# One 512-column product in place of two of 256 in the interior groups of a two-block kernel

## Chip, cores and metric

One core of a Trainium2 chip runs the whole program. The metric is device time in microseconds for one execution; less is better.

## The reference

Two transformer blocks over the same 256 tokens of 1024 features, batch 1, in fp32. The first: RMS norm, one wide input projection, gated linear attention with four heads in chunks of 64, dilated window attention with three groups of four heads, sigmoid gates and an output product, an MLP with squared ReLU (1024 to 4096 to 1024), a gated per-layer embedding, a norm. The second has two layers: SwiGLU with 2816 inner features, a convolution module (width 31) in layer 0 or multi-head latent attention in layer 1, a second SwiGLU, and a final norm. What matters here is its dense part, products of activations (256 tokens) with weights that are read once:

```
h @ w_in[i]
jnp.square(jax.nn.relu(h2 @ w_mlp1[i])) @ w_mlp2[i]
(jax.nn.silu(h @ w1) * (h @ w3)) @ w2         # four times
```

## The kernel before

**Products in three terms.** TensorE works on operands of type fp32r. To keep fp32's accuracy each operand is held as two: a rounded high part and the rest. Weights stand in `wsplit[:, slot, kk, h, :]`, activations in `xa[:, k, h, :]` or `parts[:, c, h, :]`, where h is 0 for high and 1 for rest, and the two halves lie next to each other. A product is high x high + high x rest + rest x high, three matmuls of 256 columns that add into the same place in PSUM (L535). In layout "F" the weights are stationary and the 256 tokens move; in layout "T" (the v projections) the activations are stationary and 256 weight columns move.

**Phases, groups, blocks.** The dense part is a list of phases (`add(...)`, class `Phase`). A phase's output is cut into groups of 256 output columns; a group sums over K in blocks of up to four k of 128 rows. K8 is two blocks of 4, K22 eight blocks of 3 or 2, K32 eight blocks of 4. For each k of a block and each c, one of two column blocks of 128, PE issues the three matmuls (`product_group`), after waiting for the block's weights (`lo_done`); the last of a block counts `used`. Group number G, counted through all phases, writes PSUM `ps[:, G % 2, c, 0:256]`, one bank for each c, and before it PE waits until group G - 2 has been taken (`val_done`). Groups with their kind of evacuation: gla_q and gla_k 2 each, gla_v 4, nine att phases 2 each ("keep", and "keep_tok" for v), mlp1 16 ("relu2"), mlp2 4 ("resid", K32), four up phases ffn1_up0, ffn2_up0, ffn1_up1, ffn2_up1 22 each ("swiglu"), four down phases 4 each ("resid", K22), and hr, gates, y_gla, y_att, w_out, w_pg, w_pp, pw1, pw2, mla_a, mla_kr, the uq and ukv phases, w_o and ha.

**The weights' way.** SP loads a block of up to 512 KB into one of 8 slots (L481) once the block 8 before it is used. ACT rounds it to the high part (L843, `round_block`), 5 blocks ahead of the group it belongs to; DVE subtracts to get the rest (L1057, `rest_block`), 4 blocks ahead. Both do this in the order written out in their loops: for each block of a group `ahead`, then the evacuation of that group.

**Evacuation.** DVE waits for `used` of the group's last block and reads the sum from PSUM: "keep" scales it by `rstd` (L1113), "keep_tok" by a column (L1125); a swiglu pair takes the even group as `t1 = sum * rstd` (L1138), ACT makes the silu (L901), and the odd group is multiplied with it (L1162) and split into high and rest in `parts` (L1085, L1086); "relu2" takes the maximum with 0 into `val` (L1168), squares it (L1170) and splits; "resid" of mlp2 and the down phases scales into `val` (L1189) and adds to x (L1191), which is then split with a gain (L1072, L1075). `taken()` (L1103) counts `val_done`. ACT takes no part in "keep", "keep_tok" and "relu2"; for "swiglu" it waits for DVE's `gate_in`, for "resid" for the new x. POOL adds squares for the norms; PE multiplies them with ones in plain fp32 (L560), which shows as two passes for each product. L570 are transposes, L671 products of the attention heads, all in plain fp32. DVE waits for its own last result before it uses it (`step`).

**Loops.** The middle groups of mlp1 and of the up phases are in a hardware loop on every engine (`segments`); `lin(const, coeff, i)` gives a semaphore's target in it, and `per_turn` is the number of `step`s of DVE in one turn.

## Time and profile before

| | |
|---|---|
| median of three runs | 1633.86 us (1633.27 to 1634.97) |
| the profiled execution | 1639.3 us |
| its span, first to last instruction | 1637.5 us |
| mean granted TensorE clock | 0.971 of 2.4 GHz |
| instructions | 30615 |
| HBM traffic | 257.21 MB read, 158 GB/s over the span |

The page of the profile gives busy time for each engine, the span in 40 slices, the DMA queues, the chain of work that ended last, and the costliest groups of instructions with the mean duration of one. PE's matmuls overlap: one begins before the end of the one before it, so that the distance between two starts, here called the pitch, is shorter than a duration. PEld are the weight loads, which run beside the matmuls. Lines L... are those of the kernel before.

### The profile page before, as it was taken

What the parts mean: (1) busy time and instruction counts of PE and PEld (TensorE: products, weight loads), DVE (VectorE), ACT (ScalarE), POOL (GpSimd) and SP (SyncE); (2) the same over time, 40 slices, a digit from 0 to 9 for tenths busy, and PEclk for the clock granted to TensorE, in tenths of its full rate; (3) what the DMA queues carried; (4) which work ended last, traced back from release to release, by engine and by line L of the source; (5) the groups of instructions that cost most, each with busy time, mean ns of one, the idle gap of its engine ahead of it and who ended that gap; (6) DMA issues with size and microseconds to landing.
All of it is one profiled execution on the core that took longest, in us unless ns stands there. A gap on an engine that the chain in (4) does not pass through costs nothing.

```text
span 1637.5 us, 30615 instructions
## 1 busy us (share of the span) xinstructions
PE 1565.8 (96%) x12779; PEld 1528.2 (93%) x12779; DVE 1075.9 (66%) x1333; ACT 668.9 (41%) x817; POOL 110.2 (7%) x127
## 2 busy tenths in 40 slices
PE   5989899999999998999998999999999999999995
PEld 3989899999999998999996999999999997999995
DVE  5663755559886659767694866657665687766653
ACT  3451334534333435434453534345343443443341
POOL 2000000002000005000032100000000010100000
PEclk7997999999999998999999999999999999999997
DMA  5542465445555555664642466556664653466551
GB/s 153 171 141 68 132 187 168 126 133 178 181 180 184 185 158 151 183 185 151 198 158 78 138 184 180 155 185 205 182 186 152 196 142 116 128 179 181 153 185 49
DMA packets 268213, 259.85 MB, mean 159 GB/s; under 512 B 15622, under 2 KB 267092, under 8 KB 268106
## 3 DMA queue, kind: packets, MB, share of 16 engines
q1 hardware_dynamic: 267034, 256.33, 52.1%
q0 software_dynamic: 1072, 1.98, 0.5%
q8 instruction: 81, 1.33, 0.3%
q14 instruction: 26, 0.21, 0.0%
HBM read 257.21 MB, written 1.07 MB: 158 GB/s over the span
## 4 chain that ended last, share of the span: by engine, by line
PE 57%; DVE 3%; issue 1%; ACT 0%; POOL 0%; POOLq 0%; DVEq 0%; ACTq 0%
PE ps L535 53%; PE misc L722 1%; PE misc L671 1%; DVE rstd L1093 1%; PE misc L560 0%; PE misc L570 0%; DVE parts L1075 0%; DVE wsplit L1057 0%; PE ps L697 0%; DVE plain L1438 0%; POOL acc L1555 0%; PE misc L675 0%; DVE plain L1441 0%; PE ps L692 0%; DVE plain L1118 0%
## 5 line engine op out<-in xcount | busy, mean ns | idle before, releaser
L535 PE MATMUL ps<-xa,wsplit 128*128 128x256 f32 x7104 | 872.7, 285 | 9.8 <-DVE xa L1075 5.8
L535 PEld LDWEIGHTS ps<-xa,wsplit 128*128 128x128 f32 x7104 | 864.0, 193 | 15.0 <-DVE xa L1075 6.7
L843 ACT CAST wsplit<-raw 128x1024 fp32r<-128x1024 f32 (+2 forms) x532 | 501.9, 968 | 434.8 <-DMA raw<-in_ffn_w_dram 178.4
L1057 DVE TENSOR_TENSOR wsplit<-raw,wsplit 128x1024 fp32r<-128x1024 f32 (+2 forms) x532 | 592.2, 1142 | 119.7 <-ACT wsplit L843 101.7
L535 PE MATMUL ps<-parts,wsplit 128*128 128x256 f32 x3984 | 485.8, 285 | 13.2 <-DVE parts L1086 9.0
L535 PEld LDWEIGHTS ps<-parts,wsplit 128*128 128x128 f32 x3984 | 483.0, 193 | 14.8 <-issue 8.2
L901 ACT ACTIVATE work<-t 128x512 f32<-128x512 f32 x48 | 30.4, 633 | 221.8 <-DVE t L1138 221.8
L1162 DVE TENSOR_TENSOR work<-ps,work 128x512 f32<-128x512 f32 x44 | 30.4, 691 | 76.4 <-PE ps L535 75.2
L879 ACT ACTIVATE sq<-x 128x512 f32<-128x512 f32 x40 | 25.1, 632 | 122.2 <-DVE x L1191 69.3
L1555 POOL TENSOR_TENSOR acc<-acc,sq 128x512 f32<-128x512 f32 x36 | 51.1, 1420 | 317.0 <-ACT sq L879 291.9
L1552 POOL COPY acc<-sq 128x512 f32<-128x512 f32 x14 | 9.6, 686 | 905.0 <-ACT sq L879 880.0
L1138 DVE TENSOR_TENSOR t<-ps,rstd 128x512 f32<-128x512 f32 x48 | 33.2, 691 | 56.7 <-PE ps L535 56.5
L535 PE MATMUL ps<-wsplit,xa 128*128 128x256 f32 x480 | 60.2, 289 | 5.0 <-DVEq L1103 5.0
L535 PEld LDWEIGHTS ps<-wsplit,xa 128*128 128x128 f32 x480 | 59.8, 198 | 5.2 <-DVEq L1103 5.2
L1075 DVE SCALAR_TENSOR_TENSOR xa<-x,gain,xa 128x256 fp32r<-128x256 f32 x64 | 56.1, 916 | 1.1
L1086 DVE TENSOR_TENSOR parts<-work,parts 128x512 f32 (+1 forms) x64 | 45.3, 707 | 8.6 <-DVE parts L1085 3.3
L1189 DVE TENSOR_TENSOR val<-ps,rstd 128x512 f32<-128x512 f32 x20 | 13.8, 692 | 48.1 <-PE ps L535 48.0
L1093 DVE RECIPROCAL rstd<-root 128x256 f32<-128x256 f32 x14 | 24.5, 1753 | 28.8 <-ACT root L886 28.6
L1113 DVE SCALAR_TENSOR_TENSOR plain<-ps,rstd 128x512 f32<-128x512 f32 (+1 forms) x27 | 18.3, 679 | 33.3 <-PE ps L535 33.3
L1085 DVE CAST parts<-work 128x512 f32 (+1 forms) x64 | 28.4, 444 | 11.6 <-DVE work L1162 8.8
L671 PE MATMUL misc<-plain 128*128 128x128 f32 (+3 forms) x112 | 29.4, 354 | 1.6 <-DVE plain L1308 1.6
L1125 DVE TENSOR_SCALAR plain<-ps,rstd_tok 128x256 f32<-128x256 f32 x28 | 12.3, 480 | 24.8 <-PE ps L535 24.7
(204 smaller groups left out, 699.5 us busy)
## 6 DMA issues: line engine op xcount, KB each, us to landing
raw<-in_ffn_w_dram SPq DMA_DIRECT2D x176, 512.0 KB, 3.7
raw<-in_w_in_dram SPq DMA_DIRECT2D x76, 512.0 KB, 3.6
raw<-in_ffn_w_dram SPq DMA_DIRECT2D x96, 384.0 KB, 3.1
raw<-in_w_mlp_dram SPq DMA_DIRECT2D x64, 512.0 KB, 3.6
raw<-in_conv_w_pw_dram SPq DMA_DIRECT2D x24, 512.0 KB, 3.5
raw<-in_ffn_w_dram SPq DMA_DIRECT2D x32, 256.0 KB, 2.9
raw<-in_w_o_gla_dram SPq DMA_DIRECT2D x8, 512.0 KB, 3.4
raw<-in_w_out_dram SPq DMA_DIRECT2D x8, 512.0 KB, 3.3
```

The source lines that it names most:

```text
L535: last = mm(o, still, moves, start=st and n == 0, stop=en and n == 2, skip_group_check=True)
L671: mm(o, q[:, t * P:(t + 1) * P], k[:, 0:(t + 1) * P], start=(n == 0), stop=False, skip_group_check=True)
L843: nc.scalar.copy(wsplit[:, slot, 0:kn, 0, 0:p.width], raw[:, slot, 0:kn, 1, 0:p.width]).then_inc(hi_done, 1)
L901: act_fn(gated[:, :, :], t1[:, :, :], ACT.Silu if kind == "swiglu" else ACT.Sigmoid).then_inc(gate_out, 1)
L1057: TT(wsplit[:, slot, 0:kn, 1, 0:p.width], raw[:, slot, 0:kn, 1, 0:p.width], wsplit[:, slot, 0:kn, 0, 0:p.width].bitcast(F32), ALU.subtract ...
L1075: STT(dst[:, c, 1, :], src[:, c, :], gain[:, at + c:at + c + 1], dst[:, c, 0, :].bitcast(F32), ALU.mult, ALU.subtract).then_inc(ready, 1)
L1085: step(vec.tensor_copy(dst[:, :, 0, :], src))
L1086: TT(dst[:, :, 1, :], src, dst[:, :, 0, :].bitcast(F32), ALU.subtract).then_inc(ready, n)
L1093: vec.reciprocal(dst[:, :], root[:, :]).then_inc(norm_read, 1)
L1138: TT(t1[:, :, :], total, r2, ALU.mult).then_inc(gate_in, 1)
L1162: step(TT(t2[:, :, :], total, gated[:, :, :], ALU.mult))
L1555: gp.tensor_tensor(acc[:, :, :], acc[:, :, :], sq[:, q % 2, :, :], ALU.add).then_inc(summed, 1)
```

## The change

A method `halves` names the groups that are treated in a new way: those of the phases in `WIDE`, except the last group of a phase, unless it is a keep or keep_tok phase. In such a group the first matmul of a unit (one k, one c) takes both halves of the moving operand at once, 512 columns, into the whole bank: high x high goes to the first 256 columns and high x rest to the second 256. The second matmul, rest x high, adds to the second 256. PE issues two matmuls for three, with the same number of columns. At the group's end ACT copies the second halves of both banks to SBUF (`lohalf`, two buffers), and DVE adds them to the first halves into `val`, which counts `val_done`; what follows reads `val` in place of PSUM. In mlp1 the maximum and the square are one operation for these groups. The other groups stay as they were.

```diff
@@ -71,6 +71,10 @@
 SILENT = ("conv", "ffn1_up0", )
 
+WIDE = (["gla_q", "gla_k", "gla_v", "mlp1", "mlp2"] + [f"att_{w}{g}" for w in "qkv" for g in range(3)]
+        + [f"ffn{n}_{w}{i}" for n in (1, 2) for w in ("up", "down") for i in range(2)])
+
+
 def bias_table():
 
@@ class Phase @@
         yield list(range(first, first + per)), turns
         yield list(range(first + per * turns, self.groups)), None
+    def halves(self, g):
+
+        return self.name in WIDE and (g < self.groups - 1 or self.evac[0] in ("keep", "keep_tok"))
+
     def block(self, g, j):
         return self.block0 + g * len(self.kns) + j
@@ -154,6 +162,7 @@
         xa = sb("xa", [P, NC, 2, T], F32R)
         x = sb("x", [P, NC, T])
         val = sb("val", [P, 2, T])
+        lohalf = sb("lohalf", [P, 2, 2, T])
         t1 = sb("t1", [P, 2, T])
         work = sb("work", [P, 5, T])
         t2, gated = work[:, 0:2, :], work[:, 2:4, :]
@@ -294,10 +303,11 @@
         by = {p.name: p for p in phases}
-        blocks, nblk, ngrp, ngate, nkept = [], 0, 0, 0, 0
+        blocks, nblk, ngrp, ngate, nkept, nlow = [], 0, 0, 0, 0, 0
         GATES = {"func": 1, "swiglu": 0.5, "glu": 0.5}
         for p in phases:
-            p.block0, p.group0, p.gate0, p.kept0 = nblk, ngrp, ngate, nkept
+            p.block0, p.group0, p.gate0, p.kept0, p.low0 = nblk, ngrp, ngate, nkept, nlow
+            nlow += sum(p.halves(g) for g in range(p.groups))
             nkept += p.groups if p.evac[0] in ("ha", "keep", "keep_tok") else 0
             nblk += p.groups * len(p.kns)
             ngrp += p.groups
@@ -388,6 +398,7 @@
         hi_done = sem("hi_done")
         lo_done = sem("lo_done")
         used = sem("used")
+        lohalf_done = sem("lohalf_done")
         val_done = sem("val_done")
         ready = sem("ready")
         gate_in = sem("gate_in")
@@ -523,17 +534,22 @@
                         mov = p.moving(k)
                         wboth = wsplit[:, slot, kk, :, :]
                         for c in range(p.width // P):
-                            o = ps[:, bank, c, 0:T]
+                            o = ps[:, bank, c, :]
                             st, en = k == 0, k == nk - 1
-                            if p.layout == "F":
-                                terms = [(wboth[:, w, c * P:(c + 1) * P], mov[:, m, :]) for w, m in
-                                         ((0, 0), (0, 1), (1, 0))]
+                            F = p.layout == "F"
+                            wh, wl = [wboth[:, h, c * P:(c + 1) * P] if F else wboth[:, h, :] for h in range(2)]
+                            mh, ml = [mov[:, h, :] if F else mov[:, h, c * P:(c + 1) * P] for h in range(2)]
+                            if p.halves(g):
+                                still, both = (wh, mov) if F else (mh, wboth)
+                                mm(o, still, both.rearrange("p h t -> p (h t)"), start=st, stop=False,
+                                   skip_group_check=True)
+                                still, moves = (wl, mh) if F else (ml, wh)
+                                last = mm(o[:, T:2 * T], still, moves, start=False, stop=en, skip_group_check=True)
                             else:
-                                terms = [(mov[:, m, c * P:(c + 1) * P], wboth[:, w, :]) for w, m in
-                                         ((0, 0), (1, 0), (0, 1))]
-                            for n, (still, moves) in enumerate(terms):
-                                last = mm(o, still, moves, start=st and n == 0, stop=en and n == 2,
-                                          skip_group_check=True)
+                                terms = [(wh, mh), (wh, ml), (wl, mh)] if F else [(mh, wh), (ml, wh), (mh, wl)]
+                                for n, (still, moves) in enumerate(terms):
+                                    last = mm(o[:, 0:T], still, moves, start=st and n == 0, stop=en and n == 2,
+                                              skip_group_check=True)
                     last.then_inc(used, 1)
             def conv_sum(early):
@@ -862,6 +878,14 @@
                     last = nc.scalar.copy(*shift_copy(n, h, q))
                 last.then_inc(copied_act, 1)
+            def take_lohalf(p, g, i, per):
+
+                G = p.group0 + g
+                act.wait_ge(used, lin(p.block(g, len(p.kns) - 1) + 1, RING if i is not None else 0, i))
+                if G >= 2:
+                    act.wait_ge(val_done, lin(G - 1, per, i))
+                nc.scalar.copy(lohalf[:, G % 2, :, :], ps[:, G % 2, :, T:2 * T]).then_inc(lohalf_done, 1)
+
             def square_pair(name, c, src):
                 q = pairs[name][0] + c
                 if name == "conv":
@@ -891,6 +915,8 @@
             def evacuate(p, g, i, per):
                 kind = p.evac[0]
+                if p.halves(g):
+                    take_lohalf(p, g, i, per)
                 if kind == "func":
                     n = p.gate0 + g
                     act.wait_ge(gate_in, n + 1)
@@ -1100,10 +1126,18 @@
                 def taken():
-                    v.sem_inc(val_done, 1)
-
-                v.wait_ge(used, lin(p.block(g, len(p.kns) - 1) + 1, RING if i is not None else 0, i))
-                after_split()
+                    if not p.halves(g):
+                        v.sem_inc(val_done, 1)
+
+                if p.halves(g):
+                    v.wait_ge(lohalf_done, lin(p.low0 + g + 1, per, i))
+                    after_split()
+                    TT(val[:, :, :], total, lohalf[:, G % 2, :, :], ALU.add).then_inc(val_done, 1)
+                    v.wait_ge(val_done, lin(G + 1, per, i))
+                    total = val[:, :, :]
+                else:
+                    v.wait_ge(used, lin(p.block(g, len(p.kns) - 1) + 1, RING if i is not None else 0, i))
+                    after_split()
                 if kind == "ha":
                     keep(p, g, TT(ha[0:GLA_RANK, :], total[0:GLA_RANK, 0, :], rstd[0:GLA_RANK, :], ALU.mult))
                     taken()
@@ -1165,9 +1199,12 @@
                 if kind == "relu2":
                     c = lin(2 * g, 2 * per, i)
-                    step(TS(val[:, :, :], total, 0.0, None, ALU.max))
-                    taken()
-                    step(TT(t2[:, :, :], val[:, :, :], val[:, :, :], ALU.mult))
+                    if p.halves(g):
+                        step(STT(t2[:, :, :], total, 0.0, total, ALU.max, ALU.mult))
+                    else:
+                        step(TS(val[:, :, :], total, 0.0, None, ALU.max))
+                        taken()
+                        step(TT(t2[:, :, :], val[:, :, :], val[:, :, :], ALU.mult))
                     split(parts[:, bass.ds(c, 2), :, :], t2[:, :, :], 2)
                 if kind == "times":
                     v.wait_ge(gate_out, by["gates"].gate0 + 8)
@@ -1356,7 +1393,7 @@
                     if turns is not None:
                         base, split0 = mine[0], halves[0]
                         halves[1] = {"relu2": 8, "swiglu": 4}[p.evac[0]]
-                        per_turn = {"relu2": 3 * 4, "swiglu": 2 * 2}[p.evac[0]]
+                        per_turn = {"relu2": 2 * 4, "swiglu": 2 * 2}[p.evac[0]]
                         with v.Fori(0, turns) as i:
                             loop[:] = [i, per_turn]
                             for g in groups:
```

## Rows read from the trace of the kernel before

**Rows 1.** The page of the profile: busy time by engine, clock, DMA share.
```profile
PE 1565.8 (96%) x12779; PEld 1528.2 (93%) x12779; DVE 1075.9 (66%) x1333; ACT 668.9 (41%) x817; POOL 110.2 (7%) x127
...
PEclk7997999999999998999999999999999999999997
DMA  5542465445555555664642466556664653466551
```

**Rows 2.** The chain of work that ended last: pieces in order of time.
```profile
936.10 190.06 PE ps L535 x1584
...
1430.52 168.48 PE ps L535 x1404
```

**Rows 3.** The page: the costliest group of L535.
```profile
L535 PE MATMUL ps<-xa,wsplit 128*128 128x256 f32 x7104 | 872.7, 285 | 9.8 <-DVE xa L1075 5.8
```

**Rows 4.** Who waited for whom, PE: us in total, times, longest us.
```profile
PE ps L535 <- DVEq L1103: 12.0, 5, 5.0
PE ps L535 <- DVE parts L1086: 9.0, 3, 5.5
```

**Rows 5.** Windows: an up phase, mlp1, and one at the low clock.
```profile
core 0: us, PE busy (x) PEld busy (x) DVE busy (x) ACT busy (x) POOL busy (x), PEclk, DMA share, GB/s
1200.00:1260.00 60.00, 60.00 (x502) 60.00 (x502) 35.47 (x42) 21.98 (x26) 0.00 (x0) 1.00 0.54 163
420.00:480.00 60.00, 60.00 (x502) 60.00 (x502) 50.73 (x65) 22.53 (x22) 0.00 (x0) 1.00 0.59 183
623.50:627.90 4.40, 4.40 (x23) 4.40 (x22) 4.26 (x6) 1.84 (x3) 1.29 (x1) 0.50 0.00 0
```

**Rows 6.** Groups of five short stretches: loaded, lone, lone fp32; low clock: lone, lone fp32.
```profile
L535 PE MATMUL ps<-xa,wsplit 128*128 128x256 f32 x400 | 48.2, 283 | 0.0
...
L535 PE MATMUL ps<-parts,wsplit 128*128 128x256 f32 x1 | 0.3, 279 | 0.0
...
L671 PE MATMUL misc<-plain 64*128 64x128 f32 x1 | 0.3, 272 | 0.0
...
L535 PE MATMUL ps<-xa,wsplit 128*128 128x256 f32 x1 | 0.4, 415 | 0.0
...
L570 PE MATMUL misc<-ident,plain 128*128 128x128 f32 x1 | 0.4, 418 | 0.0
```

**Rows 7.** Groups of 935.1 to 935.9 us, and PE's time line of that stretch.
```profile
L560 PE MATMUL misc<-acc,ones 128*128 128x256 f32 x4 | 1.0, 378 | 0.0
...
935.07 1.02 PE L560 MATMUL misc<-acc,ones 128*128 128x256 f32 x4
```

**Rows 8.** Groups by form over the whole span: the nearest to what is added.
```profile
L843 ACT CAST wsplit<-raw 128x1024 fp32r<-128x1024 f32 x388 | 396.4, 1045 | 303.5 <-DMA raw<-in_w_in_dram 95.8 <-DMA raw<-in_w_mlp_dram 81.5 <-DMA raw<-in_ffn_w_dram 72.7
...
L951 ACT COPY work<-misc 128x768 f32<-128x768 f32 x4 | 3.2, 802 | 0.0
...
L879 ACT ACTIVATE sq<-misc 128x512 f32<-128x512 f32 x4 | 2.4, 590 | 12.0 <-PE misc L722 12.0
...
L1189 DVE TENSOR_TENSOR val<-ps,rstd 128x512 f32<-128x512 f32 x20 | 13.8, 692 | 48.1 <-PE ps L535 48.0
```

**Rows 9.** Time line of DVE in an up phase (start us, us).
```profile
947.85 0.69 DVE L1138 TENSOR_TENSOR t<-ps,rstd 128x512 f32<-128x512 f32 x1 [1.62 <-PE ps L535]
...
953.40 0.69 DVE L1162 TENSOR_TENSOR work<-ps,work 128x512 f32<-128x512 f32 x1 [1.99 <-PE ps L535]
...
955.54 2.35 DVE L1057 TENSOR_TENSOR wsplit<-raw,wsplit 128x1024 fp32r<-128x1024 f32 x2
959.32 0.69 DVE L1138 TENSOR_TENSOR t<-ps,rstd 128x512 f32<-128x512 f32 x1 [1.42 <-PE ps L535]
```

**Rows 10.** Time line of DVE in mlp1.
```profile
424.00 0.69 DVE L1168 TENSOR_SCALAR val<-ps 128x512 f32<-128x512 f32 x1
...
429.85 0.69 DVE L1168 TENSOR_SCALAR val<-ps 128x512 f32<-128x512 f32 x1 [0.77 <-PE ps L535]
...
431.55 0.43 DVE L1085 CAST parts<-work 128x512 f32 x1 [0.16 <-DVE work L1170]
```

## The prediction

> **What bounds the kernel.** I read the page from the top. The busy shares [rows 1] put PE at 96% of a 1637.5 us span with the clock granted in full for nearly all of it; DVE stands at 66%, ACT at 41%, and the 16 DMA engines at about half. The chain that ended last [rows 2] is PE's, most of it at L535, in long pieces: one holds 1584 products in 190.06 us, another 1404 in 168.48. Both give 120.0 ns from one product to the next, without a gap. The costliest group [rows 3] is that line's largest form, with a mean of 285 ns for each product; that is the duration of one product and overlaps with the next, so it is the 120 ns that counts. The two largest of PE's waits at L535 [rows 4] are 21 us in eight pieces, against 1400 us of products. The windows [rows 5] say the same: 60 us full of L535, DVE at 35 of 60, and 51 of 60 in mlp1, where DVE is fullest. So the kernel's length is the number of products times their pitch, plus some stalls at phase changes that the change leaves alone.
>
> **What is removed.** Counted in units of one k and one column block c, L535 issues 3872 units of three products (11,616). The change halves groups of gla_q, gla_k (2 each), gla_v (4), the nine att phases (2 each), mlp1 (15 of 16), mlp2 (3 of 4), the four up phases (21 of 22) and the four down phases (3 of 4): 26, 15, 3, 84 and 12, so 140 groups. They hold 26 x 16 + 15 x 16 + 3 x 64 + 84 x 16 + 12 x 44 = 2720 units. Each has 3 x 256 = 768 columns before and after; what goes is one issue and one weight load. A window of length w shows (w + one duration) / pitch products: (60.00 + 0.283) / 502 = 0.120, and at the low clock (4.40 + 0.415) / 23 = 0.209 [rows 5, 6], which is about 256 columns at 1.2 GHz (0.213) with no excess. So at the low clock nothing is won; I take 30 units off for that: 2690.
>
> **What a product of 512 columns costs.** No row shows one of this type, so I bound it. 256 columns at 2.4 GHz are 106.7 ns; the pitch is 120.0; the excess is 13.3 ns.
> - Upper bound: two of today's, 240 ns. The unit stays at 360 and nothing is saved.
> - Lower bound: the nearest row with as many array cycles, a pass of a plain fp32 product of 256 columns (L560). Four of them span 1.02 us, the last 0.378, so the pitch is (1.02 - 0.378) / 3 = 0.214 [rows 7]. Then the unit is 214 + 120 = 334 and saves 26.
>
> Between them it matters what the 13.3 ns are. The stretches of [rows 6] split them. A product with a weight load behind it has 283 ns, one with nothing behind it 279: 4 ns belong to the load, once per load. The same comparison says that the product alone holds the array about 116 ns. An unloaded fp32 pass of 128 columns, the same 256 array cycles, has 272, so 7 of the excess are peculiar to this type at this length. Are these 7 paid per product or per column? At the low clock the lone L535 product has 415 and a lone fp32 pass of 128 columns (L570) 418: there the excess is gone, even reversed. A fixed latency should show at both clocks; columns that cannot come faster than some 0.45 ns each would show only at the high one. That speaks for columns. So 512 columns take 2 x 116 = 232, 4 for the load behind it, and 2 less for what every pass pays once (214 against the 213.3 of 512 cycles leaves 1 to 2): **234**. The unit becomes 234 + 120 = 354, a saving of **6 ns**, and 2690 x 6 = **16 us**.
>
> The Trainium skill (TensorE: Matmul & The Clock Gate, "Back-to-back issue gap") states N / 2.4 + 2.5 ns for the warm gap; by it 256 columns would take 109, where this trace shows 120, and 512 would take 216. With 216 the unit would be 336 and the change worth 65 us; the trace does not agree with the rule at 256, and no run here shows 512 of this type.
>
> **What is added.** ACT copies 128x512 from PSUM in each of 140 groups: 590 ns for the nearest form (the squares of misc), 802 for a copy of 768 columns [rows 8]; I take 0.6, in all 84 us, ACT from 669 to 753. DVE adds a 128x512 from PSUM, 692 ns like L1189 [rows 8], 97 us; mlp1's two operations (L1168, L1170) become one, which gives back 15 x 0.69 = 10. DVE goes from 1076 to about 1163 us, 71%. The operations behind the add now read SBUF instead of PSUM; I leave their durations. These all lie beside PE.
>
> **The new wait.** DVE's add now waits for ACT's copy, and ACT, which never waited for `used` at such a point, holds back behind it its next two roundings (L843), the silu, and with them DVE's L1057. The time line of a swiglu pair [rows 9] shows what there is to hide it in: L1138 and L1162 start 5.55 to 5.92 us apart, DVE idles 1.4 to 2.0 us before each. After an even group's end: copy 0.7, add 0.7, L1138 0.85, silu 0.63, one rounding 1.05 [rows 8], one L1057 1.2, together 5.1, under the 5.66 us (16 x 354 ns) of a group. After an odd one: copy 0.7, add 0.8, L1162, L1085 and L1086 about 2.1, two L1057 2.35, together 6.0, so 0.3 over, which the even group's slack returns. PE doesn't feel that: bank G's release is needed a whole group later, at 5.7 us, and comes after 1.5 (before, after 0.7); the roundings are four to five blocks, 11 us, ahead. mlp1 is tightest: L1168 to L1168 is 5.85 us with 0.77 of idle before it and 0.16 before L1085 [rows 10], so 4.9 of work; after the change it is the same work (an add and one operation in place of two), 5.1 with the short waits of DVE for its own results, and the 0.8 us for the copy makes 5.9. But a DVE that falls behind finds the copy ready and stops falling behind. Cost to PE: 0; bound, if mlp1's groups each ran at DVE's 5.9, 15 x 0.24 = 4 us. Last groups of the phases that end in a residual or a split stay as they are, so phase changes keep their stalls; gla and att phases are halved to the end, but `kept` is read one group later at the earliest, under 5.8 us of other products. Loads: a block every 2.83 us, 185 GB/s, where 183 already runs at a DMA share of 0.59 [rows 5]. SP's and POOL's queues get nothing new. No added wait stands in PE's queue beyond those it has.
>
> **Sum.** Against the profiled execution (1639.3 us, span 1637.5), 1639.3 - 16 = 1623; the median of the runs is 5.4 lower, 1633.9, so the forecast is 1633.9 - 16 = **1618**.
>
> **Rivals.**
> 1. *The excess is per product.* Then each unit saves 13.3 ns, all of the excess of the product that goes: 2690 x 13.3 = 36 us, **1598**. For it: the fp32 passes too have a small part that doesn't grow. Against: it vanishes at the low clock. 0.22.
> 2. *The 512-column stream runs clean*, as an fp32 pass of 512 cycles does: 21 to 26 ns per unit, 56 to 70 us, **1568** to 1578. Against: the lone product has its 7 ns with no load beside it. 0.15.
> 3. *Nothing*: 240 for 512 columns, or two passes of 256 inside, so that the change does to PE nothing of what it says. **1634**, within 3. 0.10.
> 4. *Slower*: the new ACT wait reaches PE. Place: PE's wait for `val_done` or `lo_done` at a group's first product, behind ACT's copy (0.6) and what it holds back. Price if wholly exposed: 0.85 us for 140 groups, 119 us, less 16: 1737; halfway 1677. It decides from 16 / 140 = 0.12 us per group on. Against: DVE's 30% idle and the four blocks in hand. 0.08.
>
> My forecast, by column, has 0.45 and spans 1610 to 1623 (4 to 9 ns per unit).
>
> **The numbers.** A measurement of this kernel tells about 0.2% from no change, 3.3 us. Faster by more: 0.45 + 0.22 + 0.15 = 0.82; within: 0.10; slower: 0.08. The range reaches down to 1570, into the clean case, and up to 1634, the case of no gain; it leaves out the slower case and the clean case's last part, some 0.13.
>
> **What would show it.** In the chain of the profile after, a long piece of L535 inside an ffn phase: 1584 products become 1116, of which 468 have 512 columns; the mean pitch over it tells 512's cost: 187.3 us for the piece if I am right, 184 if per product, 179 if clean, 190 if nothing. The lone duration of a 512 product should be near 395, not 378 to 386. PE's two largest waits at L535 should stay near 21 us; if `val_done`, shown as DVE's add, or L1057 turns up there with tens of us, rival 4 holds. DVE's busy time should be near 1163, ACT's near 753. A time below 1600 would make me wrong on the columns, one over 1637 on the wait.

## The result, and the profile after

The change makes the kernel faster: 1622.72 us, median of four runs (1620.26 to 1624.74), against 1634.33 for the kernel before, also of four (1633.27 to 1634.97). The ratio is 0.9931, with a 95% interval of 0.9916 to 0.9945: 11.6 us less, where 16 were forecast. The profiled execution of after is one of 1620.26 us (span 1618.5). It is not to be set against the profiled 1639.3 of before as it stands: a second profiled execution of the same kernel before (experiment 5) reaches the norm sum at 405.67 us 6.3 us earlier and has the same lengths behind it. Its span is 1631.2 us, 12.7 more than after's.

The page of the kernel after, busy time and clock:

```profile
PE 1540.2 (95%) x10059; PEld 1374.4 (85%) x10059; DVE 1160.0 (72%) x1458; ACT 734.9 (45%) x957; POOL 108.9 (7%) x127
...
PEclk9999999999999998999999999999999999999997
```

Against [rows 1], PE has 2720 matmuls fewer (12779 to 10059) and DVE and ACT what was added: DVE 84 us, ACT 66. The page's groups of the two products of a unit, and of the two new operations:

```profile
L544 PE MATMUL ps<-xa,wsplit 128*128 128x512 f32 x1840 | 654.3, 400 | 9.7 <-DVEq L1130 4.6
...
L547 PE MATMUL ps<-xa,wsplit 128*128 128x256 f32 x1840 | 518.1, 282 | 0.0
...
L887 ACT COPY lohalf<-ps 128x512 f32<-128x512 f32 x140 | 82.0, 586 | 295.9 <-PE ps L547 295.8
L1135 DVE TENSOR_TENSOR val<-ps,lohalf 128x512 f32<-128x512 f32 x140 | 96.7, 691 | 158.1 <-ACT lohalf L887 157.8
```

They answer to [rows 3] and [rows 8]: the copy was put at 0.6 us and has 0.586, the add at 692 ns and has 691. The 512-column product was expected near 395 ns alone; with a weight load behind each, which the prediction puts at 4 ns, the median of these 1840 is 398. The lines have moved: L535 is now L544 (512 columns), L547 (its product of 256) and L551 (the three terms of the other groups); L843 is L859, L1057 is L1083, L1162 is L1196, L1138 is L1172, L1085 and L1086 are L1111 and L1112, the norm sum L560 is L576.

Busy time can't tell the cost of a product, since matmuls overlap. The norm sums can serve as milestones: four short fp32 products at a fixed place in the order of the work. PE's time line of the kernel before at three of them (start and duration, us; a fourth is in [rows 7]):

```profile
632.11 1.03 PE L560 MATMUL misc<-acc,ones 128*128 128x256 f32 x4
...
736.75 1.02 PE L560 MATMUL misc<-acc,ones 128*128 128x256 f32 x4
...
1126.00 1.02 PE L560 MATMUL misc<-acc,ones 128*128 128x256 f32 x4
```

The same of the kernel after:

```profile
620.91 1.02 PE L576 MATMUL misc<-acc,ones 128*128 128x256 f32 x4
...
727.31 1.03 PE L576 MATMUL misc<-acc,ones 128*128 128x256 f32 x4
...
926.07 1.02 PE L576 MATMUL misc<-acc,ones 128*128 128x256 f32 x4
...
1113.89 1.02 PE L576 MATMUL misc<-acc,ones 128*128 128x256 f32 x4
```

The stretch that holds ffn2_up0 and its down phase goes from 935.07 to 1126.00 before, 190.93 us, and from 926.07 to 1113.89 after, 187.82. It holds 1584 products before, 528 units, of which 468 are now halved, so a halved unit costs 3.11 / 468 = 6.6 ns less: 353.4 instead of 360. That is the forecast's 354. But the stretch with ffn1_up0, in the same form, went from 104.64 us to 106.40: longer, where its halved groups should have made it shorter. The views of who waited for whom show why. PE's waits for the taking of a bank from 600 to 660 us (us in total, times, longest), the kernel before and then two of the kernel after:

```profile
PE ps L535 <- DVEq L1103: 5.8, 3, 2.9
```

```profile
PE ps L544 <- DVEq L1130: 2.2, 1, 2.2
PE ps L544 <- DVE val L1135: 3.5, 1, 3.5
```

The last, on DVE's add, has no counterpart before; the first is one of before's three (the other two are at L551, 3.1 us). PE's time line at that wait, kernel after:

```profile
638.62 0.28 PE L547 MATMUL ps<-xa,wsplit 128*128 128x256 f32 x1
642.40 0.49 PE L544 MATMUL ps<-xa,wsplit 128*128 128x512 f32 x1 [3.51 <-DVE val L1135]
...
645.38 0.63 PE L544 MATMUL ps<-xa,wsplit 128*128 128x512 f32 x1
...
646.02 0.63 PE L544 MATMUL ps<-xa,wsplit 128*128 128x512 f32 x1
```

The wait is paid twice: 3.5 us idle, and then some 3.3 us of products at the granted clock of 0.51 (window 643.6 to 646.9), where a unit takes 0.64 us (645.38 to 646.02) instead of 0.35. At full clock the same products would take some 1.8 us, an estimate from 3.3 / 0.64 = 5.2 units of 0.353, so that 1.5 us come on top of the 3.5: 5 us together.

In the sum over the whole run, PE's waits for the taking of a bank and for the splits, 21 us before [rows 4], are now 26.8:

```profile
PE ps L551 <- DVE parts L1112: 9.0, 3, 5.5
PE ps L544 <- DVE val L1135: 8.9, 2, 5.4
...
PE ps L544 <- DVEq L1130: 4.6, 2, 2.3
PE ps L551 <- DVEq L1130: 4.3, 3, 2.9
```

The splits have their 9.0 as before. The taking has 17.8 where it had 12.0: the new 3.5, and 2.3 in the first groups of the run (30 to 60 us), at L544 behind a taking. The second profile of the same kernel (experiment 1) doesn't have this one: its taking is 15.3 us, 3.3 more than before. The two executions differ there in PE's pace: from 36 to 42 us PE makes 38 products in the first, a 512-column one taking 0.40 us, and 23 in the second, at 0.63 us, the duration seen above at the half clock. So the 2.3 us are no standing cost of the change.

### The profile page after: what moved, and what is told of

The parts are those of the page before. It is cut to its first block, busy times and chain, and to the rows that moved or that the text cites. A ratio compares the mean times of both kernels' runs of the same rounds, so it can differ in the third digit from the quotient of the medians.

```text
span 1618.5 us, 25693 instructions
## 1 busy us (share of the span) xinstructions
PE 1540.2 (95%) x10059; PEld 1374.4 (85%) x10059; DVE 1160.0 (72%) x1458; ACT 734.9 (45%) x957; POOL 108.9 (7%) x127
## 4 chain that ended last, share of the span: by engine, by line
PE 55%; DVE 3%; issue 2%; ACT 1%; POOL 0%; POOLq 0%; DVEq 0%; ACTq 0%
PE ps L544 26%; PE ps L547 13%; PE ps L551 12%; PE misc L738 2%; PE misc L687 1%; DVE rstd L1119 1%; PE misc L576 1%; DVE wsplit L1083 0%; PE misc L586 0%; DVE parts L1101 0%; DVE plain L1475 0%; DVE parts L1111 0%; DVE val L1135 0%; POOL acc L1592 0%; PE ps L713 0%
## 5 line engine op out<-in xcount | busy, mean ns | idle before, releaser
L544 PE MATMUL ps<-xa,wsplit 128*128 128x512 f32 x1840 | 654.3, 400 | 9.7 <-DVEq L1130 4.6
L1083 DVE TENSOR_TENSOR wsplit<-raw,wsplit 128x1024 fp32r<-128x1024 f32 (+2 forms) x532 | 590.2, 1140 | 90.2 <-ACT wsplit L859 80.0
L859 ACT CAST wsplit<-raw 128x1024 fp32r<-128x1024 f32 (+2 forms) x532 | 495.1, 969 | 193.5 <-DMA raw<-in_ffn_w_dram 88.7
L547 PE MATMUL ps<-xa,wsplit 128*128 128x256 f32 x1840 | 518.1, 282 | 0.0
L544 PEld LDWEIGHTS ps<-xa,wsplit 128*128 128x128 f32 x1840 | 347.7, 189 | 95.4 <-DVEq L1130 5.2
L547 PEld LDWEIGHTS ps<-xa,wsplit 128*128 128x128 f32 x1840 | 349.8, 190 | 0.2
L544 PE MATMUL ps<-parts,wsplit 128*128 128x512 f32 x720 | 254.6, 399 | 0.0
L551 PE MATMUL ps<-parts,wsplit 128*128 128x256 f32 x1824 | 227.3, 287 | 13.2 <-DVE parts L1112 9.0
L551 PEld LDWEIGHTS ps<-parts,wsplit 128*128 128x128 f32 x1824 | 224.4, 195 | 15.1 <-issue 8.2
L887 ACT COPY lohalf<-ps 128x512 f32<-128x512 f32 x140 | 82.0, 586 | 295.9 <-PE ps L547 295.8
L1135 DVE TENSOR_TENSOR val<-ps,lohalf 128x512 f32<-128x512 f32 x140 | 96.7, 691 | 158.1 <-ACT lohalf L887 157.8
L551 PE MATMUL ps<-xa,wsplit 128*128 128x256 f32 x1584 | 201.3, 287 | 5.9 <-DVE xa L1101 4.6
L551 PEld LDWEIGHTS ps<-xa,wsplit 128*128 128x128 f32 x1584 | 195.1, 194 | 10.4 <-DVE xa L1101 5.2
L547 PE MATMUL ps<-parts,wsplit 128*128 128x256 f32 x720 | 202.2, 281 | 0.0
L544 PEld LDWEIGHTS ps<-parts,wsplit 128*128 128x128 f32 x720 | 135.3, 188 | 33.5
L547 PEld LDWEIGHTS ps<-parts,wsplit 128*128 128x128 f32 x720 | 136.0, 189 | 0.0
L544 PE MATMUL ps<-wsplit,xa 128*128 128x512 f32 x160 | 57.8, 404 | 5.4 <-DVE val L1135 5.4
```

Source lines behind the costliest of these rows:

```text
L544: mm(o, still, both.rearrange("p h t -> p (h t)"), start=st, stop=False, skip_group_check=True)
L547: last = mm(o[:, T:2 * T], still, moves, start=False, stop=en, skip_group_check=True)
L551: last = mm(o[:, 0:T], still, moves, start=st and n == 0, stop=en and n == 2, skip_group_check=True)
L859: nc.scalar.copy(wsplit[:, slot, 0:kn, 0, 0:p.width], raw[:, slot, 0:kn, 1, 0:p.width]).then_inc(hi_done, 1)
L887: nc.scalar.copy(lohalf[:, G % 2, :, :], ps[:, G % 2, :, T:2 * T]).then_inc(lohalf_done, 1)
L1083: TT(wsplit[:, slot, 0:kn, 1, 0:p.width], raw[:, slot, 0:kn, 1, 0:p.width], wsplit[:, slot, 0:kn, 0, 0:p.width].bitcast(F32), ALU.subtract ...
```

## The experiments

Ten experiments follow. The first theory: the products are worth what was forecast, and ffn1_up0's start gives some 5 us back, because DVE's add comes late there. Rivals: the evacuation costs something everywhere, or the product of 512 columns is dearer than 354 - 120.

**1. after_again**: the kernel after, unchanged, for scatter.

> The changed kernel once more, for its scatter and for a second profile. Theory A (512-column products save about 7 ns per unit, some 18 us; 5 us of that are lost again at the start of ffn1_up0, where DVE is late under POOL's conv weights): ratio 0.993 as before, PE waits 3.5 us for DVE's add near 640 us and runs at the low clock behind it. Rival R (that stall was an accident of one execution): the ratio stays but the stall is gone from this profile.

1623.47 us (1616.55 to 1630.32, six runs), ratio 0.9915 (0.9887 to 0.9942). The wait at the start of ffn1_up0 is there again, with 3.5 us; the ffn2_up0 stretch is 187.82 us again, the ffn1_up0 stretch 107.72 (106.40 in the first profile; why they differ is told ahead of experiment 7). Its profiled execution is 10 us longer than the first one (1630.3), and 6.6 of that lie in one place, the latent attention, which the change doesn't touch: the clock was 0.83 and 0.74 in two windows there. This is the scatter of this kernel, and it limits what whole times can tell.

**2. products_only**: PE as after, DVE and ACT as before, with no copy and no add, so that the kernel leaves the second halves (high x rest, rest x high) of the halved groups out of its sums.

```diff
-                if p.halves(g):
-                    take_lohalf(p, g, i, per)
...
-                if p.halves(g):
-                    v.wait_ge(lohalf_done, lin(p.low0 + g + 1, per, i))
-                    after_split()
-                    TT(val[:, :, :], total, lohalf[:, G % 2, :, :], ALU.add).then_inc(val_done, 1)
...
+                v.wait_ge(used, lin(p.block(g, len(p.kns) - 1) + 1, RING if i is not None else 0, i))
+                after_split()
...
```

> The 512-column products alone: ACT's copy and DVE's add are left out, and with them the second half of every sum in the 140 groups (high x rest and rest x high), so this computes less; mlp1's maximum and square are two operations again, as before. Theory A: the full gain of the products, 18 to 20 us, ratio 0.988 to 0.989, no stall near 640 us beyond those of the kernel before. Rival B (the products save only what was measured, 11 us, and the added work is free): ratio 0.993, as the changed kernel. Rival C (the copy and add cost at every group): over 25 us saved.

1619.5 us (1615.48 to 1621.89), ratio 0.9896 (0.9871 to 0.9921). The milestones say it more sharply than the medians: mlp1 to w_pg 182.41 us, as in the kernel after (before 185.17); the ffn2_up0 stretch 187.82, as in after; the ffn1_up0 stretch 103.13 instead of 106.40. So the evacuation costs PE nothing in mlp1 and in ffn2_up0, and 3.3 us at ffn1_up0, or 4.6 against the second profile's 107.72. At the place of the stall PE still waits 0.5 us for a taking (at 643.61 us), where before it waits for nothing: the faster products alone use up what lead there was.

**3. evacuation_only**: the three products of before in every group, but the copy and an operation in the add's place (a maximum of the sum with its own copy, which gives the sum).

```diff
-                            if p.halves(g):
+                            if False:
...
-                nc.scalar.copy(lohalf[:, G % 2, :, :], ps[:, G % 2, :, T:2 * T]).then_inc(lohalf_done, 1)
+                nc.scalar.copy(lohalf[:, G % 2, :, :], ps[:, G % 2, :, 0:T]).then_inc(lohalf_done, 1)
...
-                    TT(val[:, :, :], total, lohalf[:, G % 2, :, :], ALU.add).then_inc(val_done, 1)
+                    TT(val[:, :, :], total, lohalf[:, G % 2, :, :], ALU.max).then_inc(val_done, 1)
```

> The added work alone: three products of 256 columns as before, but ACT copies the sum (its first halves) to lohalf in the 140 groups and DVE takes the maximum of it and PSUM, which is the sum itself; all else as in the changed kernel. Theory A: 3 to 6 us slower than before (ratio 1.002 to 1.004), all of it at the start of ffn1_up0. Rival B: within 1 us, ratio 1.000. Rival C (a cost at every group end): over 10 us slower.

1640.08 us (1635.99 to 1644.95, twelve runs), ratio 1.0031 (1.0016 to 1.0047): by the ratio 5 us slower than before. The ffn2_up0 stretch stays at 190.93 us and mlp1 at 185.17; the ffn1_up0 stretch has 109.48 instead of 104.64, which is 4.8 of the 5. The new one of PE's waits from 600 to 660 us in this kernel:

```profile
PE ps L551 <- DVE val L1135: 3.2, 1, 3.2
```

The stall comes with the evacuation alone, whatever the products are.

**4. ffn1_up0_late**: the kernel after, except that the first six groups of ffn1_up0 are not halved.

```diff
+        if self.name == "ffn1_up0" and g < 6:
+            return False
...
-                ("swiglu",), loop=(2, 4, 4))
+                ("swiglu",), loop=(6, 4, 3) if (w, i) == ("ffn1", 0) else (2, 4, 4))
...
+            p.low0 -= 6 if p.name == "ffn1_up0" else 0
```

> The changed kernel with the first 6 groups of ffn1_up0 left as they were before (three products, PSUM read directly); its hardware loop then starts at group 6 with 3 turns. 96 units less are halved, which gives up 0.6 us. Theory A: the 5.3 us come back, 4 to 5 us faster than the changed kernel, ratio 0.990. Rival R: as the changed kernel, or 0.6 us slower, ratio 0.993 to 0.994.

1617.84 us (1613.31 to 1627.41), ratio 0.9901 (0.9872 to 0.9931). The ffn1_up0 stretch is 103.19 us, and no wait of PE is left in it. Those from 600 to 660 us lie ahead of it, the longest a taking:

```profile
PE ps L554 <- DVEq L1133: 6.6, 3, 3.5
```

The forecast's 1618 was this kernel's time: with the one place mended, the rest of the change brings what was worked out for all of it. The intervals of this ratio and of experiment 1's overlap, so the 5 us between the two kernels rest on the stretch and on experiment 3, not on the medians.

Why is DVE late just there? DVE's time line of the kernel after, from ffn1_up0's group 1 to its group 2 and the one behind it:

```profile
630.05 0.68 DVE L1135 TENSOR_TENSOR val<-ps,lohalf 128x512 f32<-128x512 f32 x1
630.77 1.44 DVE L1196 TENSOR_TENSOR work<-val,work 128x512 f32<-128x512 f32 x1
632.25 1.40 DVE L1111 CAST parts<-work 128x512 fp32r<-128x512 f32 x1
633.75 2.22 DVE L1112 TENSOR_TENSOR parts<-work,parts 128x512 fp32r<-128x512 f32 x1
635.89 5.78 DVE L1083 TENSOR_TENSOR wsplit<-raw,wsplit 128x1024 fp32r<-128x1024 f32 x2
641.59 0.68 DVE L1135 TENSOR_TENSOR val<-ps,lohalf 128x512 f32<-128x512 f32 x1
```

and POOL's of the same stretch:

```profile
630.36 3.00 POOL L1592 TENSOR_TENSOR acc<-acc,sq 128x512 f32<-128x512 f32 x2 [1.32 <-ACT sq L903]
633.32 12.44 POOL L1530 TENSOR_TENSOR plain<-quad,taps 128x1024 f32<-128x1024 f32 x5
```

Elsewhere in the run L1196 takes 0.69 us, L1111 0.43, L1112 0.69 and two L1083 2.35. Here they take 1.44, 1.40, 2.22 and 5.78, and each has a POOL operation beside it. Before, the same place looked like this on DVE:

```profile
640.53 0.68 DVE L1162 TENSOR_TENSOR work<-ps,work 128x512 f32<-128x512 f32 x1
641.35 0.70 DVE L1085 CAST parts<-work 128x512 fp32r<-128x512 f32 x1
642.16 1.60 DVE L1086 TENSOR_TENSOR parts<-work,parts 128x512 fp32r<-128x512 f32 x1
643.68 5.78 DVE L1057 TENSOR_TENSOR wsplit<-raw,wsplit 128x1024 fp32r<-128x1024 f32 x2
649.39 0.68 DVE L1138 TENSOR_TENSOR t<-ps,rstd 128x512 f32<-128x512 f32 x1
```

with POOL's operations of the same kind beside them:

```profile
640.36 2.85 POOL L1555 TENSOR_TENSOR acc<-acc,sq 128x512 f32<-128x512 f32 x2 [0.83 <-ACT sq L879]
643.17 8.07 POOL L1493 TENSOR_TENSOR plain<-quad,taps 128x1024 f32<-128x1024 f32 x3
```

From group 1's evacuation to group 2's it was 8.86 us before (640.53 to 649.39) and is 11.54 after. A group's products take 5.7, and this place lives on the lead that two banks give. Before, the lead was just used up; now 0.7 us are added by the add and 2 by slower operations. One row is telling: L1162 read the sum from PSUM and took 0.68 us beside POOL's L1555; its successor L1196 reads `val` from SBUF and takes 1.44 beside the same operation of POOL.

The Trainium skill (SBUF — State Buffer, "SBUF: two separate sides") says that VectorE and GpSimd share one pair of SBUF ports, which either holds alone for a whole instruction, and that two kinds of VectorE operation take part in this: those with two inputs in SBUF, against a GpSimd operation that reads SBUF, and those in a 2-port perf mode. The trace agrees for L1196. A conversion with one input (L1111, 1.40 instead of 0.43) is slowed too; whether it ran in such a mode no run here shows.

**5. before_again**: the kernel before, run as an experiment, for a second profile.

> The kernel before once more, for a second profile. If the pitch of its products is locked at 120.0 ns whatever the interruptions, it shows 190.9 us between the norm sums of the ffn phases again; if it has two states as the changed kernel shows (units of 346.7 and of 353.3 ns in different stretches of one run), some stretches here will differ from 360 ns per unit. Ratio 1.000.

1633.44 us (1631.77 to 1640.86, ten runs), ratio 1.0003 (0.9986 to 1.0019). All stretches behind 405.67 us have the lengths of the first profile within 0.03 us (the ffn stretches 190.93 both); only what lies ahead of it differs, 365.2 us against 371.3 from the norm sum at 34 us on. No second rhythm of the products shows in this kernel.

**6. conv_weights_later**: the kernel after, with POOL held back from its products for the convolution (L1530) until block 40 of ffn1_up0 is used.

```diff
+                    pl.wait_ge(used, by["ffn1_up0"].block0 + 40)
```

> The changed kernel, but POOL waits with its five conv weights (13 us of POOL work beside DVE) until block 40 of ffn1_up0's 44. Theory A1 (the stall at the start of ffn1_up0 comes from DVE's operations that now read and write SBUF alone and run at half speed beside POOL): the stall of 3.5 us and the low clock behind it go, 4 to 5 us faster than the changed kernel, ratio 0.990, and ffn1_up0 has DVE's product L1196 at 0.7 us in place of 1.4. Theory A2 (DVE is late there for the number of its operations alone): the stall stays within 1 us of 3.5, ratio 0.993.

1623.77 us (1621.28 to 1627.96), ratio 0.9936 (0.9916 to 0.9956): no gain, where one was expected. The profile shows two halves. At the start of ffn1_up0 the theory holds: the stretch is 102.62 us, the wait for L1135 is gone, and DVE's time line has only those operations slow that still have POOL's L1593 beside them:

```profile
633.47 1.44 DVE L1196 TENSOR_TENSOR work<-val,work 128x512 f32<-128x512 f32 x1
634.95 1.40 DVE L1111 CAST parts<-work 128x512 fp32r<-128x512 f32 x1
636.45 0.69 DVE L1112 TENSOR_TENSOR parts<-work,parts 128x512 fp32r<-128x512 f32 x1
637.06 2.35 DVE L1083 TENSOR_TENSOR wsplit<-raw,wsplit 128x1024 fp32r<-128x1024 f32 x2
639.33 0.69 DVE L1135 TENSOR_TENSOR val<-ps,lohalf 128x512 f32<-128x512 f32 x1
```

But the five products of POOL now lie in the next stretch (its time line), and PE waits there instead (its waits from 726 to 825 us):

```profile
733.05 11.19 POOL L1530 TENSOR_TENSOR plain<-quad,taps 128x1024 f32<-128x1024 f32 x5 [96.99 <-PE ps L547]
```

```profile
PE ps L551 <- DVE val L1135: 2.4, 1, 2.4
```

That stretch, 85.95 us in the kernel after, has 90.75: 3.8 us are won in the one stretch and 4.8 lost in the next. So the cause is shown by place, since the stall moves with POOL's work; and moving such work to another busy stretch is no cure. No run here puts it where it meets no tight evacuation.

The next two look at the products themselves. Over long stretches of the run a halved unit takes 353.3 ns, but not in all. Windows of the kernel after, L544 alone (count of the 512-column products in brackets):

```profile
650.00:720.00 70.00, 70.00 (x203) 37.75 (x203) 1.00 0.64 188
1130.00:1190.00 60.00, 60.00 (x170) 31.87 (x171) 1.00 0.63 184
```

The first of them in after_again, the same kernel:

```profile
650.00:720.00 70.00, 70.00 (x199) 37.23 (x198) 1.00 0.58 181
```

By the rule of the prediction the first gives (70.00 + 0.39) / 203 = 0.347 us for a unit, the second (60.00 + 0.40) / 170 = 0.355, the third (70.00 + 0.40) / 199 = 0.354; one product more or less in a window is 2 ns. The mean distance between the 512-column products' starts in the trace is 346.7 ns in the first stretch and 353.3 or 353.4 in the other two. So in ffn1_up0 one execution of the kernel has the one rhythm and the next has the other. This is where the two profiles' 1.3 us in that stretch come from: some 200 units at 6.7 ns. It also says what the stall costs when the rhythm is the same: 107.72 us in after_again against 102.62 in experiment 6 (171 products of 512 columns from 655 to 715 us in both, 174 in the first profile), which is 5.1 us. From 195 to 250 us both profiles of the kernel after have 160 of them and experiment 6, whose PE program is the same, has 157. PE's time line shows the two rhythms at first hand; in each pair of rows two units lie between the first and the second, 0.69 us in the one and 0.71 in the other:

```profile
699.92 0.39 PE L544 MATMUL ps<-xa,wsplit 128*128 128x512 f32 x1
...
700.61 0.39 PE L544 MATMUL ps<-xa,wsplit 128*128 128x512 f32 x1
...
1149.73 0.40 PE L544 MATMUL ps<-xa,wsplit 128*128 128x512 f32 x1
...
1150.44 0.40 PE L544 MATMUL ps<-xa,wsplit 128*128 128x512 f32 x1
```

The same instructions, at the same granted clock of 1.00, with the same form and no wait. So the code doesn't settle which rhythm a stretch has. The next runs change the order of long and short products. Their theory C is that a unit costs the same in any order, the rival L that the order picks the rhythm.

**7. short_first**: the 256-column product ahead of the 512-column one in each unit but a bank's first. This one, pairs and quads have the six unhalved groups of experiment 4, and compare with it (ffn2_up0 stretch 187.82 us, ffn1_up0 stretch 103.19).

```diff
-                                mm(o, still, both.rearrange("p h t -> p (h t)"), start=st, stop=False,
-                                   skip_group_check=True)
-                                still, moves = (wl, mh) if F else (ml, wh)
-                                last = mm(o[:, T:2 * T], still, moves, start=False, stop=en, skip_group_check=True)
+                                still2, moves = (wl, mh) if F else (ml, wh)
+                                if not st:
+                                    mm(o[:, T:2 * T], still2, moves, start=False, stop=False, skip_group_check=True)
+                                last = mm(o, still, both.rearrange("p h t -> p (h t)"), start=st, stop=en,
+                                          skip_group_check=True)
...
```

> The kernel ffn1_up0_late with the two products of a unit in the other order (256 columns, then 512) for every k but the first. Theory C (cost by columns and loads alone, whatever the order): a unit stays at 346.7 or 353.3 ns and the time at 0.990. Rival L (the two states are a phase relation that the order of the products picks): the stretches at 353.3 move to another multiple of 6.67 ns; if all go to 346.7, 10 to 14 us faster, ratio 0.982 to 0.984.

1613.84 us (1608.0 to 1616.8, five runs), ratio 0.9859 (0.9835 to 0.9882). The ffn2_up0 stretch is 186.30 us: (190.93 - 186.30) / 468 = 9.9 ns less than before for a unit, 350.1. Neither expectation was met: the cost does depend on the order, and it did not fall to 346.7. Its profiled execution, one of the longer ones, has again a slow place in the latent attention:

```profile
1340.00:1360.00 20.00, 20.00 (x72) 15.27 (x72) 11.98 (x27) 5.88 (x15) 0.00 (x0) 0.50 0.23 70
```

Here the granted clock is 0.50 for 20 us, where no window of 20 us of the kernel before fell under 0.91 in the same part. It costs 7.8 us against before's profile, and no product of 512 columns is in it.

**8. pairs**: per k the two products of 512 columns (column blocks 0 and 1) one after the other, then their two of 256.

```diff
-                                mm(o, still, both.rearrange("p h t -> p (h t)"), start=st, stop=False,
+                                wide_args = (wh, mov) if F else (mh, wboth)
+                                mm(o, wide_args[0], wide_args[1].rearrange("p h t -> p (h t)"), start=st, stop=False,
                                    skip_group_check=True)
-                                still, moves = (wl, mh) if F else (ml, wh)
-                                last = mm(o[:, T:2 * T], still, moves, start=False, stop=en, skip_group_check=True)
+                                held.append((o, (wl, mh) if F else (ml, wh)))
+                                if len(held) == 2:
+                                    for o1, (still, moves) in held:
+                                        last = mm(o1[:, T:2 * T], still, moves, start=False, stop=en,
+                                                  skip_group_check=True)
+                                    held.clear()
```

> The kernel ffn1_up0_late with the products of the two column blocks interleaved: 512, 512, 256, 256. Theory C: two units at 693 to 707 ns as before, ratio 0.990. Rival L: another multiple of 6.67 ns per unit, 340 to 360; 340 would make it 30 us faster than the kernel before at this place alone, ratio 0.973 to 0.975; 360 would take the gain away, ratio 1.000.

1603.08 us (1600.4 to 1604.6, five runs), ratio 0.9798 (0.9779 to 0.9818). This is the best version of the study, 31 us under the kernel before and faster than the kernel after. The ffn2_up0 stretch is 185.48 us, so a unit has 11.6 ns less than before, 348.4, which neither expectation had. (Its norm sums are at 919.34 and 1104.82 us.)

The order does change the cost of the unit. The profile of pairs is 8.9 us shorter than that of experiment 4; the medians are 14.8 apart, so that some of it is scatter of the clock, which in this kernel's profile stays at 1.00 in the latent attention.

**9. before_interleaved**: is it the changing of bank that helps? The kernel before, with its three terms in turn over both column blocks.

```diff
-                        for c in range(p.width // P):
...
-                            for n, (still, moves) in enumerate(terms):
...
+                        for n in range(3):
+                            for c in range(p.width // P):
...
```

> The kernel before with only the order inside a k changed: term 0 of both column blocks, then term 1 of both, then term 2 of both, so that no product writes the bank of the one ahead of it. All products stay at 256 columns. Theory C (what 'pairs' won lies in the number of changes between lengths of product): there are none here, the pitch stays 120.0 ns, an up and down phase from norm sum to norm sum stays 190.93 us, the time 1634 us, ratio 1.000. Rival B (what 'pairs' won comes from not writing the same bank twice in a row): the gain appears here too; with some 116 ns for a product the phase takes 190.93 - 1584 x 0.004 = 184.6 us or so and the run some 1600 us.

1634.26 us, ratio 1.0002 (0.9987 to 1.0016); the ffn2_up0 stretch is 190.93 us, as before. Rival B has fallen: with products of 256 columns alone, the order moves nothing, and the pitch is 120.0 ns.

**10. quads**: four products of 512 columns, then their four of 256.

```diff
-                                if len(held) == 2:
+                                if len(held) == 4 or (kk == kn - 1 and c == p.width // P - 1):
...
```

> As 'pairs', but four 512-column products (two k, both column blocks) and then their four of 256, with what is left at a block's end issued there. Theory C: a unit is x plus c for every change of length and back; 353.3 = x + c after the change and 348.4 = x + c/2 in 'pairs' give c = 9.8 and x = 343.5, so with a quarter of the changes 346, and a ffn piece takes 190.93 - 468 x 0.014 = 184.4 us (a bit more, since blocks of 3 k leave pairs over): some 184.6, the run about 1598 us. Rival B: as in 'pairs', 185.5 us and 1603 us. Rival D (the unit can't go below the 346.7 of the shorter of the two states): 184.7 at best.

1616.58 us (1608.49 to 1619.16, four runs), ratio 0.988 (0.984 to 0.992). The ffn2_up0 stretch is 186.3 us, 0.8 longer than in pairs, where theory C expected about 1 less. So theory C has fallen as well: fewer changes of length than in pairs bring no more. Most of the rest of the time over pairs is not the products': of the 11.5 us between the two profiled executions 10.2 lie in the latent attention, where quads' granted clock is 0.52 from 1340 to 1360 us. The windows from 940 to 1000 us of pairs (first) and quads, all products:

```profile
940.00:1000.00 60.00, 60.00 (x346) 52.39 (x345) 46.69 (x54) 28.54 (x36) 0.00 (x0) 1.00 0.66 186
```

```profile
940.00:1000.00 60.00, 60.00 (x343) 52.43 (x343) 46.17 (x54) 28.54 (x36) 0.00 (x0) 1.00 0.66 186
```

Three products in 60 us are the difference of the two orders; the kernel after has 342 in this window.

## Why the prediction was right, and where it was wrong

**Right: the bound.** PE's products set the length, and what a unit saves comes out at the end. In mlp1 the stretch went from 185.17 to 182.41 us, in ffn2_up0 from 190.93 to 187.82, with DVE's load up in both.

**Right: the size of a product, for most of the run.** 353.4 ns for the unit against 354. "Paid per column" gave the right number, with some luck in its parts. From start to start in the trace (168 units from 940 to 1000 us), the 512-column product takes 236 ns and the 256-column one 117, where 234 and 120 were put down: two misses of 2 and 3 ns that cancel. In the other rhythm (655 to 715 us) they take 230 and 117. As a mechanism "per column" is not shown: at 699.92 us the same unit takes 347, exactly what rival 1 (per product) priced, and pairs has 348.4. A cost fixed per column could not do that. The prediction weighed two laws as if one of them had to hold; the hardware has more than one rhythm, and the likelier of the two happened to be the commoner. Its split of the 13.3 ns into 4 for the load, 7 for the columns and the rest was read from single durations, and no run here tests those terms by themselves. At the half clock nothing is won, as it said: a unit takes 0.64 us after and 3 x 0.209 = 0.63 before. The clean stream of rival 2 (334 to 339) was seen nowhere, nor was rival 3 (360); its lower end was 1633.9 - 70 = 1564, not the 1568 that stands there. The Trainium skill's rule (TensorE: Matmul & The Clock Gate, "Back-to-back issue gap"), which that section gives for a single isolated matmul, comes to 216 ns for 512 columns; the trace agrees with it in neither rhythm (236 and 230).

**Right: ACT and DVE.** DVE was put at 1163 us and has 1160.0. ACT was put at 753 and has 734.9, though its copies sum to 82.0, near the 84 of the forecast: they overlap with their neighbours (one starts at 629.18 us for 0.57, and the next operation starts at 629.66), so a sum of durations says too much of ACT.

**Wrong: "Cost to PE: 0".** The step named mlp1 as the tightest place. It isn't. DVE's time line in mlp1, kernel after:

```profile
427.29 0.69 DVE L1135 TENSOR_TENSOR val<-ps,lohalf 128x512 f32<-128x512 f32 x1 [0.54 <-ACT lohalf L887]
...
432.94 0.69 DVE L1135 TENSOR_TENSOR val<-ps,lohalf 128x512 f32<-128x512 f32 x1 [0.53 <-ACT lohalf L887]
```

From one group to the next it is 5.65 us, 16 units of 353 ns, with half a microsecond of idle time left: PE sets the pace, as the prediction argued. The tight place was ffn1_up0's start, which the prediction covered with "phase changes keep their stalls" and "bank G's release is needed at 5.7 us and comes after 1.5". The second sentence was read from the middle of an up phase [rows 9] and is true there. At 649.39 us of before's time line the release was only just in time, beside two L1057 of 5.78 us that should have caught the eye against 2.35 in [rows 9]. It came at 650.07 us, and the group that needs it starts 48 units behind the norm sum, near 650.4: there two products of before stand 0.22 us apart once (650.25 and 650.47), in place of 0.12, so the lead was gone. A term is missing from the sum: - 5 us for this place (experiments 3 and 4, and 6 against 1). With it the sum is 11, and 11.6 were measured.

**Wrong: "the operations behind the add now read SBUF instead of PSUM; I leave their durations".** That holds wherever POOL rests; beside POOL L1196 doubled, from 0.68 to 1.44. It is part of the same missing term.

**Rival 4** had the right engine and semaphore (DVE's `val_done` at a group's first product), and the wrong place: it priced the wait in 140 groups, and it came in one, because in the stretches looked at ACT's copy and DVE's add fit under 5.7 us of products.

**Open.** What the two rhythms are, and what sets which in one execution; why pairs has 348.4, short_first 350.1 and quads 350.2. No run here tells these.

## What to carry to other kernels

When work is added behind an engine that has slack on the average, look for the place with the least lead in the time line of before: the start of phases, and wherever an operation shows two or three times its usual duration. Moving an operand from PSUM to SBUF isn't free for DVE where POOL works on SBUF beside it. And where two kinds of product share a stream, try their order: here it was worth nearly as much per unit (5.0 ns) as the change itself (6.6).

## What was not expected of the hardware

The stream of 512- and 256-column products ran at 347 or 353 ns a unit with the same code, clock and operands, for long stretches each, and the same stretch had the one in one execution and the other in the next. The 6 ns between them lie in the 512-column product (230 and 236 from start to start; the other 117 in both). Products of 256 alone ran at 120.0 in every stretch of before's kernels that was measured. Order alone took a unit to 350.1 (short first), 348.4 (pairs) and 350.2 (quads). A DVE operation on 128x512 took 1.44 us instead of 0.69 beside a POOL operation when it read SBUF alone, and kept 0.68 when it read PSUM. And the granted clock fell to half for up to 20 us in the latent attention in some executions and not in others, which cost 7.8 us in the profile of short_first against before's and is more than half of what this change brings. Such a place is in three of the eight profiles with 512-column products (after_again, short_first, quads) and in none of the four without; so few don't tell whether the change makes it likelier.
